# Loads and waits moved at the seams of a one-core decoder step, and 24 score pieces computed twice

## The reference, cut to what matters

```
z = rmsnorm(x) @ w_in                 # 1024 -> q,k,v of 8 heads A, q,k,v of 8 heads B, 8 forget logits
A, prompt: softmax(q k^T * scale + c_q - c_k, causal) @ v        # c = cumsum of log-forget ("forgetting")
B, prompt: three dilations (128,1), (512,4), (2048,16), merged by their softmax denominators ("dilated")
A, samples: the same against a paged cache of k, v and log-forget, gathered by page_table
B, samples: the same against the window buffers win_k, win_v
x1 = x + concat(A, B) @ w_o
y  = x1 + relu(rmsnorm(x1) @ w_up)^2 @ w_down                    # 1024 -> 4096 -> 1024
```

## Time and profile before

| | before |
|---|---|
| median of three executions | 3806.71 us |
| the profiled execution: its own time, its span | 3811.23 us, 3809.6 us |
| mean granted TensorE clock | 0.955 of full speed |
| busy: PE, VectorE, ScalarE, POOL | 3529.5, 1485.8, 980.6, 1111.5 us |

### The profile page before, as it was taken

The page is one execution under the profiler, slowest core; times in us unless marked ns, Lnnn a source line. Parts: engine busy times, 40 slices in busy tenths (PEclk is TensorE's granted clock), DMA queues, the critical chain, the costliest instruction groups (busy, mean ns, idle before and its releaser), DMA issues. The chain is left out here.

```text
span 3809.6 us, 50178 instructions
## 1 busy us (share of the span) xinstructions
PE 3529.5 (93%) x18192; PEld 2750.2 (72%) x18192; DVE 1485.8 (39%) x2869; ACT 980.6 (26%) x1424; POOL 1111.5 (29%) x1034
## 2 busy tenths in 40 slices
PE   7999999799998999969997799999997899999999
PEld 7987778455554677744444688888886788888898
DVE  2223323555544656333332244334433233333333
ACT  3322222244442222222222321111212311111111
POOL 2224356567665565601231200000000200000000
PEclk9999999899998999989998899999998999999999
DMA  6546666756656566378885111111104111111111
GB/s 201 193 163 199 227 199 214 190 156 179 181 143 172 159 173 186 108 293 305 300 266 169 45 61 50 44 44 44 55 28 171 51 46 40 40 42 44 44 44 61
DMA packets 303528, 507.60 MB, mean 133 GB/s; under 512 B 48850, under 2 KB 190676, under 8 KB 297940
## 3 DMA queue, kind: packets, MB, share of 16 engines
q1 hardware_dynamic: 266356, 370.29, 32.2%
q10 hardware_dynamic: 23032, 80.04, 6.2%
q0 software_dynamic: 13952, 54.80, 4.0%
HBM read 408.18 MB, written 164.50 MB: 150 GB/s over the span
## 5 line engine op out<-in xcount | busy, mean ns | idle before, releaser
L2879 DVE TENSOR_TENSOR fin_x<-mlp_y,fin_x 128x512 f32<-128x512 f32 x544 | 350.1, 685 | 746.0 <-PE mlp_y L2922 746.0
L2839 POOL TENSOR_TENSOR mlp_u<-mlp_r 128x1024 f32<-128x1024 f32 (+2 forms) x80 | 131.6, 1645 | 1327.5 <-ACT mlp_r L2780 1327.5
L2899 PE MATMUL mlp_u<-fin_h_hi,mlp_w_hi 128*128 128x512 f32 (+2 forms) x1280 | 451.2, 353 | 29.8 <-DVE mlp_w_lo L2855 29.8
L2901 PE MATMUL mlp_u<-fin_h_hi,mlp_w_lo 128*128 128x512 f32 (+2 forms) x1280 | 450.9, 352 | 0.0
L2900 PE MATMUL mlp_u<-fin_h_lo,mlp_w_hi 128*128 128x512 f32 (+2 forms) x1280 | 450.8, 352 | 0.0
L2920 PE MATMUL mlp_y<-mlp_w_hi,mlp_u_hi 128*128 128x512 f32 x1088 | 423.8, 389 | 0.8 <-DVE fin_x L2879 0.8
L2921 PE MATMUL mlp_y<-mlp_w_lo,mlp_u_hi 128*128 128x512 f32 x1088 | 424.3, 390 | 0.0
L2922 PE MATMUL mlp_y<-mlp_w_hi,mlp_u_lo 128*128 128x512 f32 x1088 | 423.9, 390 | 0.0
L676 PE MATMUL proj_z<-proj_w_lo,proj_x_hi 128*128 128x512 f32 (+1 forms) x816 | 307.1, 376 | 0.0
L675 PE MATMUL proj_z<-proj_w_hi,proj_x_hi 128*128 128x512 f32 (+1 forms) x748 | 282.9, 378 | 19.3 <-DVE proj_w_lo L520 10.7
L1046 POOL TENSOR_TENSOR fox_acc<-fox_acc,fox_pT 128x512 f32<-128x512 f32 (+3 forms) x256 | 268.8, 1079 | 61.5 <-ACT fox_pT L1093 54.7
(11 more groups left out here) (268 smaller groups left out, 6241.4 us busy)
## 6 DMA issues: line engine op xcount, KB each, us to landing
samp_k_in<-in_cache_k SPq DMA_DIRECT2D x128, 256.0 KB, 4.6
samp_v_in<-in_cache_v POOLq DMA_DIRECT2D x128, 256.0 KB, 4.7
mlp_w_raw<-in_w_up SPq DMA_DIRECT2D x64, 512.0 KB, 4.0
mlp_w_raw<-in_w_down SPq DMA_DIRECT2D x64, 512.0 KB, 4.3
out_new_win_k<-in_win_k ACTq DMA_DIRECT2D x8, 4080.0 KB
out_new_win_v<-in_win_v ACTq DMA_DIRECT2D x8, 4080.0 KB
proj_x_hi<-scratch_xt SPq DMA_DIRECT2D x34, 512.0 KB, 6.4
proj_x_lo<-scratch_xt SPq DMA_DIRECT2D x34, 512.0 KB, 6.3
```

What stands on the lines that cost most here:

```text
L2879: dve.tensor_tensor(part, y_ps[(tiles * par + t) % 2][0:rows, q * D_G:(q + 1) * D_G], part, ALU.add).then_inc(y_added, 1)
L2899: pe.matmul(out, hi, h_hi[:, k, c0:c0 + n], start=(k == 0), stop=False)
L2901: mm = pe.matmul(out, lo, h_hi[:, k, c0:c0 + n], start=False, stop=(k == KC - 1))
```

## The change

`load_fox_in` is issued at the end of pass 2. In the forgetting stage the 4 pages behind each `decay` load go, and 8 instead of 4 pages follow `load_q(p + 1, 2)`, so that a pair moves 40 pages instead of 52. The keys of group 0 of the samples are loaded in the dilated stage into memory that was its `acc`; half of `pT` of the forgetting stage lies there too. The waits for the samples' tables come later, the mask's copy one slot later. `o_in`, `w_raw` and their semaphores outlive a stage, so that the first two weight pieces of an MLP are loaded in the joining before it, and the first two `o_in` of the second joining in the first MLP; the wait for the first group's results goes to SP's start in the second joining. In pair 0 of both prompt stages the 8 pieces of m = 0 and the 16 of m = 1 are multiplied twice into the same bank.

```diff
 # project, SP
-                    if p == 2 and i == 2:
-                        ...
-                        sp.wait_ge(product, 2 * N_TILES)
-                        sp.wait_ge(squared, 2 + N_TILES)
-                        load_fox_in(sp, dram, fox_in)
 ...
                 store_zt(p, PAIRS - 1, -1)
                 if p == 1:
                     load_xt(2, 0, 0)
+                else:
+                    ...
+                    load_fox_in(sp, dram, fox_in)
                 store_z(p, PAIRS - 1, 1)
 # attend_fox, SP
                     load_decay(p + 1, x)
-                    move_pages(4)
                 scores_done(p, FOX_FIRST[3] - 1)
                 load_q(p + 1, 2)
-                move_pages(4)
+                move_pages(8)
 # attend_fox, PE (attend_dilated alike, with a loop of two)
+                if p == 0 and o < LOW_BASE[2]:
+                    pe.matmul(bank[:, 0:n], qa[m][:, z, j * P:(j + 1) * P], ka[ka_slot(p, x)][:, z, 0:n],
+                              start=True, stop=True)
 # attend_fox and attend_dilated, tiles
-        pT = ph.sb("pT", [P, PT_N, Q_COLS])
+        pT_more = ph.sb("pT", [P, PT_N // 2, Q_COLS])
+        pT = [spare[:, k // 4, k % 4, :] for k in range(PT_N // 2)] + [pT_more[:, k, :] for k in range(PT_N // 2)]
-        acc = ph.sb("acc", [P, 2, SEQ])
+        acc = samp_in["k"][:, :, :, :].rearrange("p z m t -> p z (m t)")
 # attend_dilated, SP
             load_samp_in(sp, dram, samp_in)
+            sp.wait_ge(den_done, HEAD_PAIRS * MACROS)
+            for s2 in range(2):
+                sp.dma_start(samp_in["k"][:, s2, :, :], window_rows(dram, "win_k", s2, 0))\
+                    .then_inc(samp_in["k_loaded"][s2], 16)
 # attend_samples, SP, ACT, DVE, PE
-            for G in range(N_GROUPS):
+            for G in range(1, N_GROUPS):
+            act.dma_start(new_unreached[:, :], ...).then_inc(unreached_loaded, 16)      # now first
-            dve.wait_ge(mask_loaded, 16)
-            dve.tensor_copy(unreached[:, :], unreached_in[:, 0:10 * P]).then_inc(mask_set, 1)
-            dve.wait_ge(consts, 16 * 5)
             for slot in range(SLOTS):
+                if slot == 1:
+                    dve.wait_ge(mask_loaded, 16)
+                    dve.tensor_copy(unreached[:, :], unreached_in[:, 0:10 * P]).then_inc(mask_set, 1)
+                    if G == 0:                                   # DVE, turn "n"
+                        dve.wait_ge(unreached_loaded, 16)
+                if n == 0:                                       # DVE, before the first weighing
+                    dve.wait_ge(consts, 16 * 4)
-            pe.wait_ge(consts, 16 * 5)
+                    pe.wait_ge(consts, 16 * 4)                   # PE, turn "r"
 # join_heads
-            load_o(0)
+            if g == 0:
+                load_o(0)
+            else:
+                sp.wait_ge(sent, 16 * GROUPS_T[0][1])
-                if k == KC + 4:
+                if g == 0 and k == KC + 4:
                     load_o(1)
             for t in range(2, tiles):
                 load_o(t)
+            load_mlp_in(sp, dram, w_raw_mlp, w_loaded_mlp)      # two pieces of w_up, 512 KB each
-                if k == KC:
+                if k == 2:
                     hi_o(0)                                      # and lo_o(0) alike
 # mlp, SP
-            for q in range(PIECES):
-                if q >= 2:
-                    sp.wait_ge(w_split, q - 1)
+            for q in range(2, PIECES):
+                sp.wait_ge(w_split, q - 1)
                 load(0, q)
+            if g == 0:
+                for t in range(2):
+                    load_heads(sp, dram, o_in, o_loaded, P, GROUPS_T[1][0], t)
-            sp.wait_ge(out_sent, 16 * tiles)
+            if g == 1:
+                sp.wait_ge(out_sent, 16 * (GROUPS_T[0][1] + GROUPS_T[1][1]))
 # mlp, tiles
-        r = ph.sb("r", [P, FB, 512])
+        r = spare[:, :].rearrange("p (f t) -> p f t", f=FB)
-        u_hi = ph.sb("u_hi", [P, 2, FB, 512], F32R)
+        if g == 0:
+            u_hi = ph.sb("u_hi", [P, 2, FB, 512], F32R)
+        else:
+            u_hi = o_in[:, :, 0:D_MODEL].rearrange("p s (f t) -> p s f t", f=FB)
```

More of the change, by code:

```diff
@@ L349, in _ @@
                     load_xt(2, 0, 0)
+                else:
+                    for slot in range(2):
+                        sp.wait_ge(zt_sent[slot], 32 + 32 * (TILES // 2))
+                    sp.wait_ge(c_sent, 16)
+                    load_fox_in(sp, dram, fox_in)
                 store_z(p, PAIRS - 1, 1)
@@ L1026, in _ @@
                 n = MACROS * p + m
-                tiles = [[pT[:, (4 * G + 2 * k + z) % PT_N, :] for z in range(2)] for k in range(2)]
+                tiles = [[pT[(4 * G + 2 * k + z) % PT_N] for z in range(2)] for k in range(2)]
                 if kt == 0 and n >= 2:
@@ L1743, in low_scores @@
                     pe.wait_ge(maxed, N_LOW * p + o - LOW_BANKS + 1)
-                pe.matmul(low_ps[(N_LOW * p + o) % LOW_BANKS][:, 0:n], qa[p % 2][:, z, i * P:(i + 1) * P],
-                          ka[p % 2][:, z, x * Q_COLS:x * Q_COLS + n], start=True, stop=True).then_inc(scored_low, 1)
+                for _twice in range(2 if p == 0 and o < LOW_BASE[2] else 1):
+                    mm = pe.matmul(low_ps[(N_LOW * p + o) % LOW_BANKS][:, 0:n], qa[p % 2][:, z, i * P:(i + 1) * P],
+                                   ka[p % 2][:, z, x * Q_COLS:x * Q_COLS + n], start=True, stop=True)
+                mm.then_inc(scored_low, 1)
             def turn_max(p, m):
@@ L1947, in attend_samples @@
     with Phase(nc, "samp") as ph:
-        k_in = ph.sb("k_in", [P, KV_SLOTS, 2, 4, D_G])
-        v_in = ph.sb("v_in", [P, KV_SLOTS, 2, 4, D_G])
+        k_in = [samp_in["k"]] + [ph.sb(f"k_in{k}", [P, 2, 4, D_G]) for k in range(1, KV_SLOTS)]
+        v_in = [ph.sb(f"v_in{k}", [P, 2, 4, D_G]) for k in range(KV_SLOTS)]
         kT = ph.sb("kT", [P, 2, 2, 4, 4 * P])
@@ L1998, in attend_samples @@
         mask_set = ph.sem("mask_set")
-        k_loaded = [ph.sems(f"k_loaded{k}_", 2) for k in range(KV_SLOTS)]
+        k_loaded = [samp_in["k_loaded"]] + [ph.sems(f"k_loaded{k}_", 2) for k in range(1, KV_SLOTS)]
         v_loaded = [ph.sems(f"v_loaded{k}_", 2) for k in range(KV_SLOTS)]
@@ L2439, in products @@
                         mm = pe.matmul(o_ps[half(s2), :], pT[:, G % 2, k * P + s2 * SEQROWS:k * P + (s2 + 1) * SEQROWS],
-                                       v_in[:, G % KV_SLOTS, s2, k, :], start=(q == 0 and k == 0), stop=False)
+                                       v_in[G % KV_SLOTS][:, s2, k, :], start=(q == 0 and k == 0), stop=False)
                 if part == 1 and last:
@@ L2474, in _, with join_heads @@
                     products(v, 1)
-def join_heads(nc, c, dram, g, first, tiles, h_hi, h_lo, x1):
+def join_heads(nc, c, dram, g, first, tiles, h_hi, h_lo, x1, o_in, o_loaded, w_raw_mlp, w_loaded_mlp, sent):
     with Phase(nc, f"join{g}") as ph:
@@ L2523, in load_o @@
             def load_o(t):
[L2524 removed]
                 if t >= 2:
                     sp.wait_ge(o_turned, t - 1)
[L2527 to L2528 removed]
+                load_heads(sp, dram, o_in, o_loaded, rows_of[t], first, t)
             def load_w(k):
@@ L2684, in _, with mlp @@
             turn_h(tiles - 1)
-def mlp(nc, c, dram, g, first, tiles, h_hi, h_lo, x1):
+def mlp(nc, c, dram, g, first, tiles, h_hi, h_lo, x1, w_raw, w_loaded, o_in, o_loaded, spare, out_sent):
     tokens = min(tiles * P, (TILES - first) * P + N_SAMPLE)
@@ L2944, in _, with load_mlp_in, load_heads, finish @@
             body(BLOCKS - 1, 1, False)
-def finish(nc, c, dram):
-    for g, (first, tiles) in enumerate(((0, TILES // 2), (TILES // 2, TILES // 2 + 1))):
-        with Phase(nc, f"fin{g}") as ph:
-            tokens = min(tiles * P, TILES // 2 * P + N_SAMPLE)
-            h_hi = ph.sb("h_hi", [P, KC, tokens], F32R)
-            h_lo = ph.sb("h_lo", [P, KC, tokens], F32R)
-            x1 = ph.sb("x1", [P, tiles, D_MODEL])
-            join_heads(nc, c, dram, g, first, tiles, h_hi, h_lo, x1)
-            mlp(nc, c, dram, g, first, tiles, h_hi, h_lo, x1)
+def load_mlp_in(sp, dram, w_raw, w_loaded):
+    for q in range(2):
+        src = dram["w_up"][q * KC // 2 * P:(q + 1) * KC // 2 * P, 0:FBLK].rearrange("(k p) f -> p k f", p=P)
+        sp.dma_start(w_raw[:, q, :].rearrange("p (k f) -> p k f", f=FBLK), src).then_inc(w_loaded[q], 16)
+def load_heads(sp, dram, o_in, o_loaded, n, first, t):
+    sp.dma_start(o_in[0:n, t % 2, 0:D_MODEL].bitcast(F32), dram["att"][(first + t) * P:(first + t) * P + n, :])\
+        .then_inc(o_loaded[t % 2], 16)
+GROUPS_T = ((0, TILES // 2), (TILES // 2, TILES // 2 + 1))
+def finish(nc, c, dram, ph, o_in, spare):
+    sent = ph.sem("out_sent")
+    o_loaded = [ph.sems(f"o_loaded{g}_") for g in range(2)]
+    for g, (first, tiles) in enumerate(GROUPS_T):
+        w_loaded = ph.sems(f"w_loaded{g}_")
+        with Phase(nc, f"fin{g}") as tile:
+            tokens = min(tiles * P, TILES // 2 * P + N_SAMPLE)
```

(6 more changed lines are left out.)

42 lines of the change are left out of this document (18 added, 24 removed).

## The result

The changed kernel takes 3786.75 us, the median of six executions (3781.53 to 3794.27), against 3806.86 for the kernel before: a ratio of 0.9949 (95% interval 0.9936 to 0.9963). It is faster, as forecast, but by 20 us (0.5%) where 42.5 were summed, and lies 4.8 us above the range of 3752 to 3782. Its profiled execution took 3782.47 us with a span of 3780.8, 28.8 us less than the span before. Two later executions, one of the changed kernel and one of the kernel before, took over 10200 us each, and all medians and ratios here leave them out.

A forecast was written before the change was run, and what follows sets the result against it. PE, busy in 93% of the span, bounds the kernel; time is won where it stands or runs at the lower clock. 11.7 + 8.0 + 14.2 + 0 + 7.5 + 2.1 - 1.0 = 42.5 us, giving 3764, range 3752 to 3782.

The forecast's parts named there:

- the loads out of pass 2: Projection, pass 2: moving `load_fox_in` to its end removes the standing for x and slow matmuls; 11.7 us, range 8 to 11.7.
- the MLPs' starts: Both seams before the MLPs: first weight pieces loaded ahead let ScalarE start with the stage; 7.5 us, range 6 to 8.
- the joinings: First joining: 0 us, ends -1 and +2; second joining's start: earlier first loads, 2.1 us, ends 0.5 and 4.
- Both signs: Signs of error: PE's waits reappear a few us later at the same seam, DMA named; MLP matmuls exceed 390 ns.
- "I take 14.2" at the samples' start: Samples' start: PE starts at about 1634, 14.9 us back, less 0.7 for the mask's copy; range 5.1 to 15.
- The first rival: Samples' start: full DMA engines make PE stand for third key group or first values; 5.1 instead of 14.2, 3773; chance 0.16.
- Pages, 8.0: Forgetting stage, pair 0: q goes out 15 to 19 us earlier, ending a 5.61 us stall, plus 2.4 of slow matmuls.
- 24 pieces twice, -1: Forgetting and dilated stages: doubled pieces mostly hidden by VectorE, perhaps bringing full clock sooner; -1 us, ends -8 and +5.
- The slower rival: MLPs: tiles in earlier stages' memory lengthen matmuls; at 4% it is 59 us, 3823; chance 0.04.
- 0.2 over, 1.6 for eight: Doubled pieces: two half-clock matmuls take 0.85 us against VectorE's 0.65 per piece, leaving this cost in us.

The follow-up runs named there:

- lf_first: Changed kernel with ScalarE's queue issuing the log-forgets' loads ahead of the four tables and the pick table: median 3775.93 us, ratio 0.9933.
- o_sb4: Changed kernel with four output slots instead of two in the dilated stage: median 3788.81 us, ratio 0.9954.
- no_double: Changed kernel with the 24 pieces computed once in both stages: 3793.6 us, one execution.
- best2: Changed kernel with single pieces, log-forgets first, four output slots, u_hi in one row 64 B further into its old memory: median 3762.35 us, ratio 0.9903.

## Why the prediction was wrong, point by point

The direction was right, and most steps with it: the loads out of pass 2 (9.1 us in the table, 10.7 over the twelve profiles with the new place, for 11.7), the MLPs' starts (8.2 for 7.5), the joinings (3.0 together for 2.1, though a joining that the change had not touched differed by 3 us between profiles). Both signs that the prediction named for being wrong came: a wait of PE a few us later at the same seam with a DMA named, and products of the MLPs above 390 ns. The range failed on four terms.

- *"I take 14.2" at the samples' start* failed by the sentence "Queued behind VectorE's new waits are only the emptying of turns and the first weighing". The first turn did come 14.9 us sooner, but I followed the five tables whose wait was moved and not the loads behind them on the same queue. The log-forgets stand last there, and PE's fixed order wants them 24 to 25 us into the stage; in the three profiles with the old start PE never waits for them. What was next late was not group 1's keys. Measured: 5.0 us of gain in the mean of two profiles, with 2.3 to 14.0 us of new waiting in nine, which two loads moved on their queue took away (lf_first).
- In the same step, a collision was looked for on the far side of the seam only. The 2 MB also collide with the stores at the end of the dilated stage: a wait of 3.5 us, some 2 net (o_sb4). The first rival, that transfers take the gain back, had the right kind of cause and the wrong loads.
- *Pages, 8.0.* The size was near where the stall falls: the two profiles of the kernel before are 7 to 9 us apart at the ends of pairs 0, 1 and 2 of the forgetting stage (158.3 for 149.0, 269.2 for 260.9, 381.3 for 374.6 us behind its start). The step that failed is "It is late because SP is busy with pages". From q's issue at 802.63 to the need at 815.4 there were 12.8 us, and the first of its two loads took 5.1. Only the second was late, behind a copy on another queue, which the earlier trace rows do not show: they are SP's alone. In the second profile of the kernel before the stall is not there, so the mean has half of it.
- *24 pieces twice, -1.* It costs some 3 us in the forgetting stage (no_double and the other single profiles against the doubled ones), which takes what was left of the pages' gain there, and nothing in the dilated one. The working "0.2 over, 1.6 for eight" plus small pieces was near; what I then set against it, denser matmuls that bring the full clock sooner, did come, but in nine of ten profiles the clock did not stay. The rule that activity releases the clock, which the prediction cited from the Trainium skill, "TensorE: Matmul & The Clock Gate", Part 1, agrees with the 0.66 for 0.50 in the first window.
- *The slower rival* named the mechanism that did come, MLP tiles in earlier stages' memory, with "place has not mattered so far" against it, and gave it a price of 59 us and no place in the sum. It came as 0.6% of the second MLP, 4.8 us, and not by the memory but by where slots start in it. The earlier trace rows could not exclude it: all its operands were tiles of their own.

Together: 14.2 to 5.0, 8.0 and -1 to 0.7 and 1.1 (with the dilated stage's 7.5 us of variation between profiles), 0 to -5.8 for the MLPs, of which the first one's -1.0 is within its variation (698.0 to 700.7 over all profiles). The sum rested on one profile of a kernel whose prompt stages vary by 7 to 12 us from one profile to another, which the three times shown, 6.8 us apart, hinted at.

## What to carry to other kernels

When a load or a wait is moved so that an engine starts sooner, list every load that the engine's next turns want, in the order of its queue, and ask of each whether it had only been on time because the engine was late. A stall that ends on a DMA may be there in one execution and not in the next: compare the load's time from issue to need with what such a load takes elsewhere, look at all queues in that stretch, and at a second profile. When a tile is laid into a leftover of another shape, compare the time of its products with that of before, and if they are longer, try other starts and strides of its slots.

## What the runs showed of the hardware that was not expected

- Moving where a stationary operand's slots start, by 32 and 64 B, changed 512-column matmuls from 390 to 395 ns each, and also products next to them whose stationary operand is another tile (392 to 394); the second MLP went from 776.6 us (best2, 64 B in, slots 4096 B apart) to 781.4 (start of the memory, 4128 B apart) by that alone.
- Loads of 256 KB issued 0.1 to 0.8 us behind a 4080 KB copy of another queue landed in 16.3 to 17.7 us, and such loads issued 0.3 to 5.8 us ahead of it in 4.5 to 5.1 (eight loads in four profiles).
